# A two-block network on one core: latents normalised in the joint stage, loads ahead at later seams, joint dense tiles in blocks of 512, 512 and 256

## What is computed

```python
# layer 0 (ab), over the 1024 tokens and, with other modulation, over 256 context tokens
h = x * (1 + sc) + sh
z = h @ w_in;  a, ga, u, v, gb = split(z)
ya = multiscale_pool(a) * silu(ga)          # four groups, windows 2, 4, 8, 16
yb = chunk_sgu(u, v) * silu(gb)             # four heads, chunks of 128
x  = layer_norm(ALPHA * x + gate * (concat(ya, yb) @ w_out))
# layer 1 (cd)
f_in, f_gate, cq, ckv, kr, d_gate = split((x * (1 + sc) + sh) @ w_in)
q    = rotate(rms_norm(cq) @ w_q_up)                # 256 latents -> 8 heads of 64 + 32
k, v = rms_norm(ckv) @ w_kv_up, with rotate(kr)     # 128 latents, 1024 + 256 keys
attn = softmax(q k / sqrt(96)) v
y    = concat(fft2(f_in).real @ w_f * silu(f_gate), attn * silu(d_gate)) @ w_out
out  = layer_norm(ALPHA * x + gate * y)
```

## Time and profile before

| | |
|---|---|
| median of 3 runs | 3363.9 us (3354.69 to 3372.49) |
| the profiled execution | 3360.23 us, its span 3358.4 us |
| TensorE busy | 3116.7 us, 93% of the span |
| weight loads busy | 2888.6 us, 86% |
| VectorE busy | 1987.1 us, 59% |
| ScalarE busy | 937.9 us, 28% |
| GpSimd busy | 151.0 us, 4% |
| mean granted TensorE clock | 0.962 |

### The profile page before, as it was taken

The page is one execution under the profiler, slowest core; times in us unless marked ns, Lnnn a source line. Parts: engine busy times, 40 slices in busy tenths (PEclk is TensorE's granted clock), DMA queues, the critical chain, the costliest instruction groups (busy, mean ns, idle before and its releaser), DMA issues. The chain is left out here.

```text
span 3358.4 us, 47720 instructions
## 1 busy us (share of the span) xinstructions
PE 3116.7 (93%) x20182; PEld 2888.6 (86%) x20182; DVE 1987.1 (59%) x2836; ACT 937.9 (28%) x1315; POOL 151.0 (4%) x124
## 2 busy tenths in 40 slices
PE   7999999999877999999999998999898977999887
PEld 7999999998867999999999998999898964555565
DVE  6666776675777446763564466444545526766446
ACT  5222232222454112211111112111323324444323
POOL 0000000000000000000000000000030001222200
PEclk9999999999988999999999999999898988999898
DMA  4233232334464334113113214111121330000221
GB/s 147 86 97 97 87 106 93 121 108 137 139 119 133 103 125 151 51 51 130 59 51 110 85 39 156 46 46 40 57 70 65 131 126 0 1 1 1 84 87 69
DMA packets 101822, 285.74 MB, mean 85 GB/s; under 512 B 13540, under 2 KB 32484, under 8 KB 100328
## 3 DMA queue, kind: packets, MB, share of 16 engines
q1 hardware_dynamic: 101608, 282.69, 26.3%
HBM read 218.79 MB, written 63.85 MB: 84 GB/s over the span
## 5 line engine op out<-in xcount | busy, mean ns | idle before, releaser
L2049 PE MATMUL joint_dense<-rst_norms_operand_b_high,joint_whigh 128*128 128x342 f32 (+2 forms) x1056 | 344.3, 326 | 17.9 <-DVEq L2166 10.5
L2049 PE MATMUL joint_dense<-rst_norms_operand_b_high,joint_wlow 128*128 128x342 f32 (+2 forms) x1056 | 341.0, 323 | 0.0
L2049 PE MATMUL joint_dense<-irst_norms_operand_b_low,joint_whigh 128*128 128x342 f32 (+2 forms) x1056 | 340.0, 322 | 0.0
L1484 PE MATMUL flow_dense<-rst_norms_operand_b_high,flow_whigh 128*128 128x342 f32 x792 | 253.0, 319 | 0.4 <-DVE flow_wlow L1579 0.4
L1484 PE MATMUL flow_dense<-irst_norms_operand_b_low,flow_whigh 128*128 128x342 f32 x792 | 252.6, 319 | 0.0
L1484 PE MATMUL flow_dense<-rst_norms_operand_b_high,flow_wlow 128*128 128x342 f32 x792 | 252.5, 319 | 0.0
L478 PE MATMUL mixer_in_dense<-mix_z_high,dense_whigh 128*128 128x348 f32 x664 | 220.1, 332 | 15.4 <-DVE dense_wlow L572 10.5
L2049 PEld LDWEIGHTS joint_dense<-rst_norms_operand_b_high,joint_whigh 128*128 128x128 f32 x1056 | 201.8, 191 | 23.4 <-DVEq L2166 8.4
L478 PE MATMUL mixer_in_dense<-mix_z_high,dense_wlow 128*128 128x348 f32 x664 | 217.5, 328 | 0.0
L478 PE MATMUL mixer_in_dense<-mix_z_low,dense_whigh 128*128 128x348 f32 x664 | 217.0, 327 | 0.0
L478 PE MATMUL mixer_in_dense<-mix_z_high,mixer_in_whigh 128*128 128x348 f32 x648 | 211.9, 327 | 0.0
(11 more groups left out here) (594 smaller groups left out, 7640.1 us busy)
## 6 DMA issues: line engine op xcount, KB each, us to landing
dense_weights<-w_in SPq DMA_DIRECT2D x56, 512.0 KB, 4.8
mixer_in_mod_w<-w_mod SPq DMA_DIRECT2D x64, 384.0 KB, 3.6
dense_weights<-w_up SPq DMA_DIRECT2D x44, 512.0 KB, 3.3
dense_tile<-h SPq DMA_DIRECT2D x24, 512.0 KB, 4.7
h<-flow_out SPq DMA_DIRECT2D x24, 512.0 KB, 3.5
dense_weights<-ab_w_in SPq DMA_DIRECT2D x20, 512.0 KB, 3.3
p<-dense_tile SPq DMA_DIRECT2D x16, 528.0 KB, 2.7
dense_tile<-p SPq DMA_DIRECT2D x16, 513.0 KB, 4.3
```

The costliest lines, as they stand in the source:

```text
L1484: mm = pe.matmul(o, w[n % NW][:, P * k:P * (k + 1)], x[h][:, k, where], start=k == 0 and e == 0, stop=k == kt - 1 and e == 2)
L2049: mm = pe.matmul(pd[s % 2][:, 0:wide], a[n % 2][:, P * k:P * (k + 1)], m, start=k == 0 and e == 0, stop=k == DT - 1 and e == 2)
```

## The change

Six things are changed together. The joint stage's tiles of all kinds but z are cut into two blocks of 512 tokens and one of 256 context columns, which takes the extra columns; the offsets of the side pieces are written anew for three slots a tile. The latents are loaded back in the joint stage's z tiles, squared, summed, normalised and, for the rotary rows, rotated; the query latents stay in SBUF, and key latents and rotated rows go to memory. The first head's q and k weights are loaded there too. `attend` loads the prepared latents and no longer waits for them ahead of q, and loads the first two inputs and the feature table of `fourier`. `fourier` loads the first two output weights and splits the first; `normed_out` begins with them. In `heads_out` the nine transfers move from slot 15 to slot 16, behind the weights of tile 7.

```diff
@@ heads_out, SP
-                    if s == 15:
+                    if s == 16:
@@ second_schedule
-        slots += [(n, b) for b in range(3 if kind == "z" else 4)]
+        slots += [(n, b) for b in range(3)]
...
-        for n, d in (("bias_v", 4), ("inverse_counts", 5), ("turn", 6), ("pad", 6), ("stats", 7), ("bias_a", 8),
-                     ("deviation", 8), ("tree", 9), ("difference", 10), ("scale_v", 11), ("bias_ga", 12), ("pool", 12),
-                     ("mix", 13), ("pooled", 14), ("mixed", 15), ("bias_u", 16), ("times_u", 17)):
+        for n, d in (("bias_v", 3), ("inverse_counts", 4), ("turn", 5), ("pad", 5), ("stats", 6), ("bias_a", 6),
+                     ("deviation", 7), ("tree", 7), ("difference", 8), ("scale_v", 8), ("bias_ga", 9), ("pool", 9),
+                     ("mix", 10), ("pooled", 11), ("mixed", 11), ("bias_u", 12), ("times_u", 13)):
...
+    s = first["z", 1] + 1
+    add(s, "latents", 0)
+    add(s + 3, "latents", 1)
+    add(s + 7, "squares", 0)
+    add(s + 8, "rope", 0)
+    add(s + 9, "latent_sums", 0)
+    add(s + 9, "put_rope", 0)
+    add(s + 12, "latent_roots", 0)
+    add(s + 15, "latent_roots", 1)
+    add(s + 16, "latent_norm", 0)
+    add(s + 17, "put_latent", 0)
@@ second_front, columns_of
-            if b == 3:
-                return slice(SEQ, T2), CTX
-            return slice(BW * b, min(SEQ, BW * (b + 1))), (BW if b < 2 else 344 if kind in ("kv", "z") else
-                                                           340 if kind == "o" else 342)
+            if kind == "z":
+                return slice(BW * b, min(SEQ, BW * (b + 1))), BW if b < 2 else 344
+            if b == 2:
+                return slice(SEQ, T2), CTX + {"kv": 4, "o": 0}.get(kind, 2)
+            return slice(512 * b, 512 * (b + 1)), 512
@@ second_front, ScalarE / TensorE / VectorE
+                        elif piece == "squares":
+                            act.wait_ge(cq_in, 64)
+                            act.wait_ge(ckv_in, 80)
+                            act.wait_ge(centred, 6)
+                            for k in range(QL // P):
+                                act.activation(cq_square[k], cq[k], ACT.Square).then_inc(latent_squared, 1)
+                            act.wait_ge(posted, 1)
+                            act.activation(sqb, ckv, ACT.Square).then_inc(latent_squared, 1)
...
+                        elif piece == "latent_sums":
+                            pe.wait_ge(latent_squared, 3)
...
+                        elif piece == "rope":
+                            dve.wait_ge(ckv_in, 80)
+                            ch.inc(tt(krt[COS, :], kr[SIN, :], turn[SIN, :], ALU.mult))
+                            ch.do(tt(kr[COS, :], kr[COS, :], turn[COS, :], ALU.mult))
+                            ch.do(tt(kr[COS, :], kr[COS, :], krt[COS, :], ALU.add))
+                            dve.sem_inc(key_turned, 1)
@@ attend, SP
+                sp.dma_start(turn[NOPE:P, 0:SEQ], t["rope"][NOPE:P, 0:SEQ]).then_inc(turn_in, 16)
+                sp.dma_start(ckv[:, :], t["latent"][:, :]).then_inc(ckv_in, 16)
+                sp.dma_start(kr[A, :], t["key_rope"][:, :]).then_inc(kr_in, 16)
+                for dst, src in ((wv[:, :], t["w_v_up"]), (wq[:, :, :, :], t["w_q_up"]), (wk[:, :, :], t["w_k_up"])):
+                    sp.dma_start(dst, src).then_inc(weights_in, 16)
                 for m in range(4):
                     sp.dma_start(dg[:, m, :], z[10 + m]).then_inc(gates_in, 16)
+                for h in range(2):
+                    sp.dma_start(shared["stage"][h][:, :], z[h]).then_inc(features_in, 16)
+                sp.dma_start(shared["dft_features"][:, :], t["dft_features"]).then_inc(features_in, 16)
@@ attend, TensorE
-                pe.wait_ge(normed, 3)
-                pe.wait_ge(landed[1], 80)
                 for n in first:
+                    if n == ("k", 0, 0):
+                        pe.wait_ge(ckv_in, 16)
                     make(n)
...
                     if s == 0:
+                        pe.wait_ge(weights_in, 48)
@@ attend, VectorE (ScalarE alike)
+                dve.wait_ge(turn_in, 16)
+                for n in first[0:2]:
                     low(n)
+                key_rope_low(0)
+                for n in first[2:]:
+                    low(n)
+                key_rope_low(1)
@@ fourier
+                sp.wait_ge(act_freed, 6)
+                for j in range(2):
+                    sp.dma_start(stage[j][:, :], t["cd_w_out"][j]).then_inc(shared["out_weights"][j], 16)
...
+                        if m == 0:
+                            act.wait_ge(shared["out_weights"][0], 16)
+                            act.activation(wh[:, :], stage[0][:, :], ACT.Copy).then_inc(high_ready, 1)
...
+                        if m == 0:
+                            dve.wait_ge(high_ready, 1)
+                            ch.do(tt(wl[:, :], stage[0][:, :], wh[:, :].bitcast(F32), ALU.subtract))
@@ normed_out
-                load(0)
-                load(1)
...
-                high(0)
+                act.sem_inc(high_ready, 1)
...
-                low(0)
+                dve.sem_inc(low_ready, 1)
```

More of the change, by code:

```diff
@@ L1732, in second_schedule @@
         if m + 2 < DT:
[L1733 removed]
+            add(s + 2, "side", m + 2)
         if m + 1 < DT:
[L1735 removed]
+            add(s + 3, "sums", m)
     x = last["o", DT - 1] + 1
@@ L1783, in w @@
             return ph.sb(name, (P, n))
-        xc = [ph.sb(f"context_{n}", (P, DT, CTX), F32R) for n in ("high", "low")]
+        xc = [ph.sb(f"context_{n}", (P, DT, CTX + 4), F32R) for n in ("high", "low")]
         wh = [ph.sb(f"whigh{j}", (P, DT * P), F32R) for j in range(2)]
@@ L1867, in _ @@
                                 sp.dma_start(t["cdz"][k], ring[j][:, 0:SEQ]).then_inc(stored[j], 16)
+                        elif piece == "latents" and i == 0:
+                            sp.wait_ge(stored[2], 16)
+                            sp.wait_ge(stored[0], 32)
+                            for dst, src in ((cq[0], t["cdz"][8]), (cq[1], t["cdz"][9]), (qn[:, :], t["q_norm"]),
+                                             (kn[:, :], t["kv_norm"])):
+                                sp.dma_start(dst, src).then_inc(cq_in, 16)
+                        elif piece == "latents":
+                            sp.wait_ge(stored[1], 16)
+                            sp.wait_ge(centred, 4)
+                            for dst, src in ((ckv, t["cdk"][0]), (kr[NOPE:P, :], t["cdk"][1][NOPE:P, :]),
+                                             (turn[NOPE:P, :], t["rope"][NOPE:P, :]),
+                                             (shared["wq"][:, :, :], t["w_q_up"][:, :, 0, :]),
+                                             (shared["wk"][:, :], t["w_k_up"][:, 0, :])):
+                                sp.dma_start(dst, src).then_inc(ckv_in, 16)
+                        elif piece == "put_rope":
+                            sp.wait_ge(key_turned, 1)
+                            sp.dma_start(t["key_rope"][:, :], kr[COS, :]).then_inc(rope_stored, 16)
+                        elif piece == "put_latent":
+                            sp.wait_ge(latent_normed, 1)
+                            sp.dma_start(t["latent"][:, :], ckv).then_inc(latent_stored, 16)
                         elif piece == "put_x2":
@@ L2026, in _ @@
                             mm.then_inc(sums_ready, 1)
+                        elif piece == "latent_sums":
+                            pe.wait_ge(latent_squared, 3)
+                            pe.wait_ge(posted, 1)
+                            for b, c0, n in pieces(SEQ):
+                                for k in range(QL // P):
+                                    pe.matmul(ps[:, c0:c0 + n], c["ones"][:, :], cq_square[k][:, c0:c0 + n], start=k == 0,
+                                              stop=k == QL // P - 1)
+                            for b, c0, n in pieces(T2):
+                                mm = pe.matmul(pt[:, c0:c0 + n], c["ones"][:, :], sqb[:, c0:c0 + n], start=True, stop=True)
+                            mm.then_inc(latent_summed, 1)
                     if s >= NS:
@@ L2201, in _ @@
                             dve.sem_inc(posted, 1)
+                        elif piece == "rope":
[4 more added lines that the diff above has]
+                            dve.sem_inc(key_turned, 1)
+                        elif piece == "latent_norm":
+                            dve.wait_ge(latent_rooted, 4)
+                            for k in range(QL // P):
+                                ch.inc(stt(out=cq[k], in0=cq[k], scalar=qn[:, k:k + 1], in1=cq_root, op0=ALU.mult,
+                                           op1=ALU.mult))
+                            ch.do(stt(out=ckv, in0=ckv, scalar=kn[:, 0:1], in1=sqb, op0=ALU.mult, op1=ALU.mult))
+                            dve.sem_inc(latent_normed, 1)
                         elif piece == "restore":
@@ L2878, in normed_out @@
     with Phase(nc, "last") as ph:
```

(25 more changed lines are left out.)

188 lines of the change are left out of this document (89 added, 99 removed).

## The result

| | before | after |
|---|---|---|
| device time, median of 4 runs, us | 3360.4 (3354.7 to 3372.5) | 3324.4 (3318.3 to 3326.5) |
| ratio | | 0.9889, 95% interval 0.9874 to 0.9903 |
| profiled execution, us | 3360.2, span 3358.4 | 3326.5, span 3324.7 |
| TensorE's mean granted clock | 0.962 | 0.968 |

What follows compares the result with a forecast made beforehand. TensorE's nearly full stream and its waits were taken as the bound. Terms of -10.8 -5.3 +7.1 +5.6 -30.4 -3.8 -6.1 -7.3 gave -51 us: 3309 profiled, 3313 against the 3363.9 median; range 3297 to 3333, own case 3301 to 3325.

Steps and rivals of the forecast that it cites:

- the three seams: Starts of attention, Fourier and last phase: earlier loads and latents shorten TensorE's waits by 30.4, 3.8 and 6.1 us.
- rival (a): Joint stage's front falls further behind, `difference` and `scale_v` in the shortest slot: 3320, or 3327 with falling clock; chance 11%.
- (b): Transfers at the starts of attention, Fourier and last phase come late, in one burst after the barrier: 3325; chance 8%.
- (c): Fewer, wider matmuls in the joint stage save only a couple of nanoseconds each: 3322; chance 4%.
- the front's new offsets: Joint stage, groups of 15 slots instead of 20: `pool` waits for `difference` four times, 8.2 us, net +7.1 us.
- Narrower against wider blocks: Joint stage: 24 matmuls fewer in each of 30 tiles, 0.36 us a tile, -10.8 us.
- Three places where a wider block fills a wait: Joint stage's start, first o tile, first kv tile: wider blocks fill TensorE's waits, -5.3 us, between -2 and -6.
- The sums: Joint stage: 14 matmul instructions for the latents' two sums, 0.43 us each, +5.6 us that no cover hides.
- rival (d): Latents' moved chain isn't hidden: TensorE waits in the joint stage's z tiles, +18, 3331; chance 6%.
- `heads_out`: Slot 15 to 16: tile 7's weights come sooner, stall 2.6 instead of 7.9 us, clock holds (2 us), -7.3 us.
- Start of attention: q starts at once on normalised latents and preloaded weights; scores at 2762.9 instead of 2793.3, -30.4 us.
- rival (e): Granted clock falls in the attention loop, making the kernel slower than before, 3373 at clock 0.84; chance 3%.

Runs made afterwards that it cites:

- Experiments 8: After kernel with the feature table's allocation lengthened from 129 to 160 columns, no instruction changed: 3324.5 us.
- 9: After kernel with 64 unused bytes ahead of the joint stage's operand and 64 behind it: 3325.1 us, ratio 0.9891.
- experiment 12: After kernel with the feature table's allocation lengthened to 384 columns, no instruction changed: one execution of 3323.7 us.
- 13: After kernel with 320 unused bytes ahead of the joint stage's operand and 832 behind it: one execution of 3322.5 us.
- experiments 4: After kernel plus eight unread matmuls behind the joint stage, two among the key blocks, and an early Exp: 3323.4 us.
- 7: After kernel with the first head's q and k weights not loaded ahead: 3332.2 us, ratio to before 0.9917.
- experiment 2: Kernel before with only the joint stage's new tiles and front offsets, without the latents: 3357.6 us, ratio 0.9989.
- Experiment 3: After kernel with `pool` moved from offset 9 to 11, `pooled` from 11 to 12: 3313.1 us, ratio to before 0.9862.
- experiment 1: Kernel before with only the `heads_out` edit, nine transfers issued behind tile 7's weights: 3354.9 us against 3360.7, ratio 0.9989.
- experiment 10: After kernel with `pool` at 10, `mix` at 11, more unread matmuls at attention's start, early Exp, GpSimd adding query squares: 3303.6 us, ratio to before 0.9829.
- 14: Kernel of experiment 10 with three unread matmuls moved ahead of the wait for the latent: 3304.1 us, ratio to before 0.9840.

## Why the prediction held within its range and promised too large a gain

The direction, the three seams and the places of the waits were right, and so were the signs named ahead: q 0.05 us after SP's first issue, the scores 16.3 us after it, four waits of `pool` that grow with the group, none in the z tiles. The size was not: 36 us against 51. 3324.4 lies 0.6 us inside the 3301 to 3325 of the forecast's own case, and it is as near to the 3320 to 3327 of rival (a), the 3325 of (b) and the 3322 of (c), so the total tells none of them apart; the traces do. The 3313 was counted from a median of 3363.9 for the kernel before; from its 3360.4 above it would be 3309 and the miss 15 us, so 3.5 us of the agreement are luck. The step that failed most is **the front's new offsets**, with **the narrower blocks** beside it. Term by term, in the profiled executions:

- **Narrower against wider blocks**, -10.8 forecast, -6.4 measured. The 512-column matmul was priced at the 227 ns of the last phase; in the joint stage it takes 230.2 (mean of some 1350), and the context's went from 119.8 to 121.2 with its two extra columns. A tile went from 14.17 to 13.96 us, not to 13.8: 30 x 0.21 = 6.4. Experiments 8, 9, 12 and 13 show that this pace moves by up to 2% with where the tiles lie, in kernels of identical instructions. The estimate of 1.8 us from the Trainium skill's page "TensorE: Matmul & The Clock Gate", section "Back-to-back issue gap", does not agree with the trace either: the 6.4 us lie midway between it and the forecast. A matmul fewer is worth 9 ns (6.4 us over 720), not the 15 of the forecast and more than rival (c)'s couple; (c) falls as it was said, but part of its doubt was right.
- **Three places where a wider block fills a wait**, -5.3 forecast, -6.7 measured (start -2.5, first o -2.3, first kv -1.9: time in these blocks and the gaps behind them over that of undisturbed ones).
- **The front**, +7.1 forecast, +11.5 measured in the profiled execution; about +10 where group 3's stand kept the clock (4.4 us instead of 5.7 around its `pool`, in experiments 4, 7, 8, 12 and 13; not in 2 and 9). The waits were priced rightly: 7.8 against 8.2, less 1.1 that went. The other 4.8 us are mostly matmuls at half clock behind the stands of 2.1 and 3.6 us. Rival (a) had the clock in it; the forecast's own case hadn't. Experiment 3 gave nearly all of it back by two offsets (9.7 us of the joint stage in the profiled executions, 11.3 in the medians).
- **The sums**, +5.6 forecast, +5.4 measured. That the rest of the latents is hidden held in every point; rival (d) falls.
- **`heads_out`**, -7.3 forecast, -5.8 measured: the wait as said, the clock not (experiment 1). The stand of 2 to 3 us is there (2.45), but in the after kernel ahead of tile 5; ahead of tile 7, where it was forecast, 1.16 is left.
- **Start of attention**, -30.4 against -30.8. What the new chain did to its successor was not priced: TensorE comes to the scores less busy, and at half clock in all seven profiles with the chain of the after kernel and no fillers; with the old start at full clock in two of three (experiment 2 was the third, and its scores took 352.4 us against 351.0 and 349.6). So the fuller stream of experiments 10 and 14 is shown to keep the clock, and what lost it in each case is not. And the removed root no longer leaves the Exp table behind. That is the +3.5 (experiment 10 took it out again).
- **The last phase**, 0 forecast, +1.5 measured: the placement of its tiles (experiment 12 took it out).
- Rival (b), late transfers, came true only in small: the token table was waited for 2.2 us instead of 1. Of rival (e) there is nothing: the granted clock in attention's loop is 0.98 to 1.00.

The misses are 4.4 + 4.4 + 1.5 + 3.5 + 1.5 = 15.3 us against me, and 1.4 + 0.2 + 0.4 + 0.4 = 2.4 for me: 12.9. With the drift of 4.4 ahead of `heads_out` that is the 17 us by which the profiled after kernel (3326.5, the slowest of its four) missed its 3309; the medians missed by 11.4.

## What to carry to other kernels

Price a stand as the wait plus what runs at half clock behind it: here stands of 2.5 us and more cost 1.5 to 3 us on top; the one of 2.1 ahead of the third group's `pool` cost 1.3 to 1.6 on top in three executions and nothing in five. When work is moved away from ahead of a phase, list what it left behind for that phase, a busy TensorE and a loaded activation table included. And when blocks get wider, the slots of an order written by hand get fewer and unequal: count each consumer's distance to its producer in time, not in slots, and keep the longest producer away from the shortest slot.

## What the hardware did that I had not expected

- The pace of a full TensorE stream depends on the tiles' places in SBUF: 226.9, 230.5, 231.2 ns for the last phase's 512-column matmul, with only the length of an unused tail changed; 230.2 or 232.0 in the joint stage, with only unused bytes around the operand. It repeats to 0.1 ns over kernels. Which addresses are good isn't settled.
- Matmuls that nobody reads can be worth their issue: eight ahead of a barrier cut q from 6.17 to 3.67 us, and eight among the keys kept the scores at full clock, while two didn't.
- In `heads_out`, over the 13 profiles, half clock followed each stand of TensorE of 1.8 us and more (1.83, 2.07, 2.08, then 2.45 and up), and none of those of 1.1 to 1.6 us. The length alone doesn't decide: at the joint stage's start the kernel before stood 2.29 us and kept full clock.
